# Gated DeltaNet stage of a two-layer trunk: silu through one Tanh, and inverse roots by Newton steps on GpSimd

## The reference, cut to what matters

```python
qkv = jax.nn.silu(causal_depthwise_conv(proj[..., :GDN_QKV_W], conv_w))
z = proj[..., GDN_QKV_W:GDN_QKV_W + GDN_VAL_W]
q = l2norm(q) * (GDN_DK ** -0.5)     # x * rsqrt(sum(x * x) + L2_EPS)
k = l2norm(k)
...
tmat = eye + a_low                   # beta * (k k^T) * decay below the diagonal
sol = triangular_solve(tmat, rhs)    # u, w
def step(s, inp):
    v_new = u_c - w_c @ s
    o_c = qd_c @ s + qk_c @ v_new
    s = s * dl_c + kd_c.T @ v_new
    return s, o_c
...
o = rmsnorm(o, o_norm) * jax.nn.silu(z)
```

## Time and profile before

| | us |
|---|---|
| median of 3 runs | 2728.78 (2727.26 to 2729.28) |
| profiled execution, its own time | 2729.88 |
| its span, first to last instruction | 2728.1 |
| mean granted clock of TensorE in it | 0.962 |
| PE busy | 2479.6 (91%) |
| DVE busy | 1671.6 (61%) |
| ACT busy | 1129.3 (41%) |
| POOL busy | 454.4 (17%) |
| the stage's later steps, each | 40.2 |
| its steps with a meta pass, each | 50.7 to 52.0 (steps 2 to 6) |

### The profile page before, as it was taken

How to read it: one execution, slowest core, us unless ns; L and a number is a source line. 1 busy time by engine, 2 the same in 40 slices (tenths; PEclk the granted TensorE clock), 3 DMA queues, 4 the chain that set the end, 5 groups by cost and what they waited for, 6 DMA issues and landing times. The chain is left out here.

```text
span 2728.1 us, 46465 instructions
## 1 busy us (share of the span) xinstructions
PE 2479.6 (91%) x17193; PEld 2186.3 (80%) x17193; DVE 1671.6 (61%) x3906; ACT 1129.3 (41%) x3326; POOL 454.4 (17%) x341
## 2 busy tenths in 40 slices
PE   5468888899999999999999689999998999999997
PEld 4467877789999999999999568878886777777775
DVE  4367777777777777777777333333333667666674
ACT  4244554544444444444444244423332333333332
POOL 0043343310000000000000012100000333323331
PEclk8689999999999999999999689999998999999998
DMA  6665454344544454444353067744456222222221
GB/s 188 199 211 171 157 189 154 118 144 156 180 141 133 157 172 158 133 155 141 125 175 100 20 216 254 249 161 143 172 201 235 105 71 87 88 71 78 70 71 49
DMA packets 274337, 395.36 MB, mean 145 GB/s; under 512 B 80066, under 2 KB 188178, under 8 KB 273714
## 3 DMA queue, kind: packets, MB, share of 16 engines
q1 hardware_dynamic: 241314, 371.25, 40.7%
q10 hardware_dynamic: 32800, 21.17, 2.6%
HBM read 268.95 MB, written 123.95 MB: 144 GB/s over the span
## 5 line engine op out<-in xcount | busy, mean ns | idle before, releaser
L1232 PE MATMUL p_psp<-xg,p_whi 128*128 128x264 f32 x4096 | 842.4, 295 | 24.4 <-POOL p_wlo L1181 17.2
L1232 PEld LDWEIGHTS p_psp<-xg,p_whi 128*128 128x128 f32 x4096 | 655.2, 191 | 28.6 <-issue 26.3
L1232 PE MATMUL p_psp<-xg,p_wlo 128*128 128x264 f32 x2048 | 606.8, 296 | 0.0
L1232 PEld LDWEIGHTS p_psp<-xg,p_wlo 128*128 128x128 f32 x2048 | 391.4, 191 | 0.0
L984 DVE SCALAR_TENSOR_TENSOR p_acc<-p_proj,p_taps,p_acc 128x528 f32<-128x528 f32 x288 | 244.7, 850 | 4.6
L1857 PE MATMUL first_q<-first_w,p_o 128*128 128x512 f32 (+1 forms) x864 | 206.1, 397 | 15.1 <-DVE first_w L1821 15.1
L2403 PE MATMUL first_q<-first_w,p_hT 128*128 128x512 f32 x720 | 194.3, 409 | 11.4 <-DMA p_hT<-hT_dram 11.4
L1857 PEld LDWEIGHTS first_q<-first_w,p_o 128*128 128x128 f32 (+1 forms) x864 | 156.6, 183 | 57.9 <-issue 13.6
L2403 PE MATMUL p_pso<-p_wo,p_oT 128*128 128x512 f32 x768 | 194.6, 404 | 7.9 <-DVE p_oT L2314 4.2
L865 ACT ACTIVATE p_sig<-p_sig 128x528 f32<-128x528 f32 x128 | 82.5, 645 | 282.0 <-DVE p_sig L986 282.0
L1857 PE MATMUL p_psz<-p_wk,p_o 128*128 128x512 f32 x768 | 181.3, 392 | 0.0
(11 more groups left out here) (264 smaller groups left out, 4637.2 us busy)
## 6 DMA issues: line engine op xcount, KB each, us to landing
p_whi<-w_dram SPq DMA_DIRECT2D x92, 512.0 KB, 4.0
p_wlo<-w_dram SPq DMA_DIRECT2D x92, 512.0 KB, 4.8
raw<-w_a_in SPq DMA_DIRECT2D x36, 512.0 KB, 6.6
w_dram<-p_whi SPq DMA_DIRECT2D x34, 512.0 KB, 3.9
w_dram<-p_wlo SPq DMA_DIRECT2D x34, 512.0 KB, 5.0
p_o<-hT_dram SPq DMA_DIRECT2D x34, 512.0 KB, 4.8
hT_dram<-p_hT SPq DMA_DIRECT2D x32, 512.0 KB, 3.4
p_hT<-hT_dram SPq DMA_DIRECT2D x30, 512.0 KB, 4.4
```

Of the source, the lines that this page charges most:

```text
L1232: ins = nc.tensor.matmul(ps_p[half_][:, 0:HALF], (w_hi, w_lo)[i][:, f, kc * P:(kc + 1) * P], xg[:, g % 2, j, kc, half_ * HALF:(half_ + 1) ...
```

## The change

Five things change, all within `gated_deltanet`.

- The sigmoid's three passes and the clamp are replaced by one pass of Tanh with scale 0.5 on ScalarE; the product becomes (tanh + 1) times x on VectorE, which is twice the silu. The factors of two are taken out later (0.25 with the squared norm of the keys, four times the epsilon, half the output gain). The products of f = 2 and f = 3 run on VectorE in every step, and the products' slots move: f = 0 from 11 to 10, f = 1 from 21 to 20, f = 2 from slot 0 of the next step to 23, f = 3 from 5 to 3.
- Inverse square roots are no longer Ln and Exp on ScalarE. VectorE writes a seed from the bits of the argument, and GpSimd does three Newton steps of four linked operations each (`inverse_root`): root_k for |k|, in slot 16 (18 in steps with a meta pass), with one more product; root_o for the outputs, in slot 12 (16). 1/|k|^2 becomes a reciprocal on VectorE.
- The scaling of the outputs becomes a stage of its own on ScalarE, slot 14 (18), and close and store move from 16 and 18 to 17 and 19 (20 and 22). The meta pass has root_o, scale, close and store in slots 1, 4, 6, 8, where norm, close and store stood in 0, 2 and 4.
- The roots lie in tiles of their own, one for each kind and pass (`root`, and `n2` for the squared norm).
- The meta pass's outputs lie in the PSUM bank `ps_t`, which also takes the transposes of the inverse, instead of `ps_o1`. PE's wait for the close of the meta pass moves from the second ks to the second left.

The diff, cut to its core:

```diff
-        TAPS = {7: (0, 0, (0, 1)), 8: (0, 0, (2, 3)), 9: (0, 0, (4,)), 13: (0, 1, (0,)), 14: (0, 1, (1,)),
-                16: (0, 1, (2,)), 18: (0, 1, (3,)), 19: (0, 1, (4,)), 20: (0, 2, (0, 1)), 21: (0, 2, (2, 3)), 22: (0, 2, (4,)),
-                1: (1, 3, (4,))}
-        SIGMOID = {9: (0, 0, (0,)), 10: (0, 0, (1, 2)), 19: (0, 1, (0,)), 20: (0, 1, (1, 2)), 22: (0, 2, (0,)),
-                   23: (0, 2, (1, 2)), 1: (1, 3, (0,)), 2: (1, 3, (1, 2))}
-        SILU = {11: (0, 0), 21: (0, 1), 0: (1, 2), 5: (1, 3)}
+        TAPS = {7: (0, 0, (0, 1)), 8: (0, 0, (2, 3)), 13: (0, 1, (0,)), 14: (0, 1, (1,)),
+                16: (0, 1, (2,)), 18: (0, 1, (3,)), 20: (0, 2, (0, 1)), 21: (0, 2, (2, 3))}
+        TANH = {9: (0, 0), 19: (0, 1), 22: (0, 2), 1: (1, 3)}
+        SILU = {10: (0, 0), 20: (0, 1), 23: (0, 2), 3: (1, 3)}
...
-                    put(2, "close", b[0], 0)
-                    put(4, "store", b[0], 0)
+                    put(1, "root_o", b[0], 0)
+                    put(4, "scale", b[0], 0)
+                    put(6, "close", b[0], 0)
+                    put(8, "store", b[0], 0)
...
-                put(16, "close", main, 0)
-                put(18, "store", main, 0)
+                put(20 if main.with_meta else 17, "close", main, 0)
+                put(22 if main.with_meta else 19, "store", main, 0)
...
                 for q in p:
+                    put(18 if q.with_meta else 16, "root_k", q, 0)
+                for q in p:
...
                 put(12, "norm", b[-1], 0)
+                put(16 if b[-1].with_meta else 12, "root_o", b[-1], 0)
+                put(18 if b[-1].with_meta else 14, "scale", b[-1], 0)
...
@@ -1062,14 +1047,19 @@
                                                               nD[par][:, p.which, c:c + 1], e_g[:, p.ix(c), :],
                                                               ALU.mult, ALU.mult)
                     last.then_inc(low_ready, 1)
+                    if not zero(p.first):
+                        dve.wait_ge(vs_ready, p.first)
+                    link(nc.vector.tensor_scalar(root[:, 0, p.which, 0, 0:n], squared, -0.5, None, ALU.mult))
+                    nc.vector.tensor_scalar(root[:, 0, p.which, 1, 0:n].bitcast(i32), squared.bitcast(i32), -0.5, float(ROOT_SEED),
+                                            ALU.mult, ALU.add).then_inc(norm_seeded, 1)
                 elif stage == "vs":
                     dve.wait_ge(v_ps, k + 1)
-                    dve.wait_ge(norm_ready, 2 * k + 2)
+                    dve.wait_ge(norm_ready, k + 1)
                     nc.vector.tensor_tensor(v_s[par][:, at, :], chunks(ps_t if p.meta else ps_k)[:, 0:n, :], bc(norm[:, p.which, 0:n], n),
                                             ALU.mult).then_inc(vs_ready, 1)
...
@@ -1116,8 +1106,11 @@
                 elif stage == "norm":
                     dve.wait_ge(state_ready, p.chunk + n)
                     dve.wait_ge(oss_ready, p.chunk + n)
-                    nc.vector.scalar_tensor_tensor(o_ms[:, 0:n], o_ss[:, 0:n], 1.0 / P, o_bias[par][:, p.which, 0:n],
-                                                   ALU.mult, ALU.add).then_inc(ms_ready, 1)
+                    link(nc.vector.scalar_tensor_tensor(o_ms[:, 0:n], o_ss[:, 0:n], 1.0 / P, o_bias[par][:, p.which, 0:n],
+                                                        ALU.mult, ALU.add))
+                    link(nc.vector.tensor_scalar(root[:, 1, p.which, 0, 0:n], o_ms[:, 0:n], -0.5, None, ALU.mult))
+                    nc.vector.tensor_scalar(root[:, 1, p.which, 1, 0:n].bitcast(i32), o_ms[:, 0:n].bitcast(i32), -0.5, float(ROOT_SEED),
+                                            ALU.mult, ALU.add).then_inc(ms_seeded, 1)
...
+            links = [0]
+
+            def link(ins):
+                links[0] += 1
+                ins.then_inc(pool_chain, 1)
+                pool.wait_ge(pool_chain, links[0])
+
+            def inverse_root(kind, p, last=None):
+
+                minus_half, y, t = (root[:, kind, p.which, x, 0:p.n] for x in range(3))
+                for turn in range(ROOT_STEPS):
+                    link(nc.gpsimd.tensor_tensor(t, y, y, ALU.mult))
+                    link(nc.gpsimd.tensor_tensor(t, t, minus_half, ALU.mult))
+                    link(nc.gpsimd.tensor_scalar(t, t, 1.5, None, ALU.add))
+                    step_done = nc.gpsimd.tensor_tensor(y, y, t, ALU.mult)
+                    if turn == ROOT_STEPS - 1 and last is not None:
+                        step_done.then_inc(last, 1)
+                    else:
+                        link(step_done)
+                return y
...
+                elif stage == "root_k":
+                    pool.wait_ge(norm_seeded, k + 1)
+                    y = inverse_root(0, p)
+                    nc.gpsimd.tensor_tensor(norm[:, p.which, 0:p.n], n2[:, p.which, 0:p.n], y, ALU.mult).then_inc(norm_ready, 1)
+                elif stage == "root_o":
+                    pool.wait_ge(ms_seeded, k + 1)
+                    inverse_root(1, p, last=ms_ready)
...
+                pool.sem_clear(pool_chain)
+                links[0] = 0
                 for slot in schedule(it, p, a, b, splitting):
                     for stage, q, index in slot.stages:
                         stage_of(stage, q, index, b)
-                    for q, item, f in slot.silu:
-                        if f >= 2 and splitting[1]:
-                            silu(q, item, f, b)
...
                     if index:
+                        if index == 1 and b and b[0].meta:
+                            pe.wait_ge(o_g_ready, b[0].number + 1)
...
-                        if index == 1 and p.with_meta:
-                            pe.wait_ge(o_g_ready, k)
```

More of the change, by code:

```diff
@@ L884, in stage_of @@
                     act.wait_ge(k_ps, k + 1)
+                    if not zero(k):
+                        act.wait_ge(scaled, k)
                     for c in range(n):
@@ L888, in stage_of @@
                     last.then_inc(k_squared, 1)
-                elif stage == "kk":
-                    l = lnk[:, p.which, 0:n]
-                    act.wait_ge(k_squared, k + 1)
-                    link(nc.scalar.activation(l, ssq[:, p.which, 0, 0:n], ACT.Ln, bias=cst[:]))
-                    if not zero(k):
-                        act.wait_ge(scaled, k)
-                    if not zero(p.first):
-                        act.wait_ge(vs_ready, p.first)
-                    nc.scalar.activation(rn2[:, p.which, 0:n], l, ACT.Exp, scale=-1.0).then_inc(norm_ready, 1)
-                    nc.scalar.activation(norm[:, p.which, 0:n], l, ACT.Exp, scale=0.5).then_inc(norm_ready, 1)
                 elif stage == "tokQ":
@@ L929, in stage_of @@
                         nc.scalar.activation(o_n[:, c, :], o_of(p, c), ACT.Copy,
-                                             scale=o_ms[:, c:c + 1]).then_inc(o_read, 1)
+                                             scale=root[:, 1, p.which, 1, c:c + 1]).then_inc(o_read, 1)
                 elif stage == "store":
@@ L1323, in stage_of @@
                         pe.wait_ge(qk_ready, k + 1)
+                        if p.meta and a and a[0].meta:
+                            pe.wait_ge(vs_ready, a[0].number + 1)
                         if p.leading:
```

126 lines of the change are left out of this document (49 added, 77 removed).

## The result

The changed kernel takes 2740.15 us (median of 5 runs, 2731.42 to 2745.34) against 2728.78 on the same chip: a ratio of 1.004, 95% interval 1.003 to 1.0051. The forecast of 2709.8 was wrong, on the wrong side of no change, and the measured time lies just past the end of its range (2740.0). The profiled execution of after is the lowest of its five runs (2731.42, span 2729.6), so the trace shows a loss of only 1.5 us in the span; what the other runs add is taken up with the first experiment.

What follows compares the result with a forecast made beforehand. PE's matmuls were taken to set the time, so only PE's waits could be won. Later steps -24, opening and steps 8, 9 -4, early +6, end +3 give -19; 2729.9 - 19 - 1.1 = 2709.8 us, range 2693 to 2740.

Steps and rivals of the forecast that it cites:

- three signs of being wrong: Links taking 0.4 us, the inverse's load waited for 22 times, or the early steps getting shorter.
- Later steps, -24: Steps 10 to 31: PE's waits for keys and state go, 1.1 us a step over 22 steps; bounds -11 to -31.
- the load of the inverse would not follow: Rival, chance 0.16: in later steps the inverse's DRAM load lands late, leaving some 0.3 us a step; 2727.
- The link, 0.28 us: One dependent small GpSimd operation of the inverse roots takes 0.28 us; bounds 0.18 and 0.51.
- The end, +3: Last step: 0.66 us from o_ms to first scaling becomes two seeds, 0.4 us, and 12 links, 3.4; bounds +2 and +5.
- Opening steps, -3: Steps 0 and 1: each saves two sigmoid passes and a clamp, partly taken back by VectorE's work; -1 to -6.
- Steps 8 and 9, -1: These two steps win half a microsecond each.
- Early steps, +6: Steps 2 to 7: per step -3.0 ScalarE, +2.3 VectorE, +1.7 GpSimd, so +1.0; bounds -11 to +33.
- ScalarE's relief: Early steps: waits for w and evacuations, and half of those for vT, go; -3.0 us a step.
- 310.6 + 38 s reaches 322.3 at s = 0.31, so 0.28 just fits: Early steps: 38 links of s us after a weight split ending at 310.6 must finish before the values' scaling at 322.3.
- 12 small operations: Early steps: VectorE's added squared norm, reciprocal and seed work, priced at 0.15 us each and a hand-off.
- The link is dear: Rival, chance 0.20: links cost more, nothing won at 0.43 us, 2746 at 0.47, about 2766 at 0.51.

Runs made afterwards that it cites:

- a0_again: The first experiment: the changed kernel run once more, nothing altered; 2740.48 us, ratio 1.0042.
- e1: The changed kernel with the outputs' root ahead of the keys' root in steps 8 and 9; 2732.23 us, ratio 1.0014.
- e6: The changed kernel with the main keys' seeds put behind the addition into p_X in early steps; 2734.36 us, ratio 1.0023.
- e9: The changed kernel with one Newton step instead of three and the main keys' seeds behind the addition into p_X; 2702.45 us, ratio 0.9908.
- e3: The changed kernel with root_o in slot 12 and the meta keys' root in 13, ahead of the weight splits; 2709.57 us, ratio 0.9933.
- e8: The kernel before the change with five idle linked VectorE operations ahead of the second addition into p_X in meta-pass steps; 2742.17 us, ratio 1.0056.
- e10: The changed kernel with e3's root order, plus qT product and solve rows 4, 5, 6 behind the first r in early steps; 2679.9 us, ratio 0.9824.
- e4: The changed kernel with one Newton step instead of three, so 14 links instead of 38; 2723.51 us, ratio 0.998.

## Why the prediction was wrong, point by point

The sum was to be -19 against the profiled execution; its span grew by 1.5, and the median lies 8.7 us above that execution. Two terms failed, the early steps by 13 us and steps 8 and 9 by 7; in a0_again, whose profile lies near its median, these stretches lost even 22.8 and 9.3. None of the three signs of being wrong that the prediction named came true: links of 0.4 us, an inverse waited for 22 times, shorter early steps.

- **Later steps, -24: right** (-25.2; 39.1 us each, as forecast). Keys and state left the waits of PE. That the load of the inverse would not follow, a rival, did not happen: after waits for it 3 times in 22 steps, 1.4 us in all.
- **The link, 0.28 us: right where nothing disturbs it** (12 links from 780.29 to 783.90 in step 13, 0.30 with one of them stretched by 0.25). The Trainium skill, "GPSIMD Engine Reference", section 4.1, led to an estimate of 0.38; the trace gives 0.28 alone, and 0.37 in the early step, where it is the waiting for VectorE and not the work that is longer (0.99 and 0.20 for the same operation).
- **The end, +3: right.** From `p_oms` to the first scaling 4.0 us (1555.35 to 1559.39) instead of 0.66, +3.4; 3.8 us had been forecast, and the rest of the span grew by 2.0.
- **Opening steps, -3, measured -1.1**: within the bounds given (-1 to -6).
- **Steps 8 and 9, -1: failed, +6.3.** I had looked at the root of the outputs in the later steps and in the early ones, and not in these two, where both roots stand in slot 16 and the keys' comes first (e1: -8 us in the median, and these steps back at 88.5).
- **Early steps, +6: this term failed; +19.4** (inside its own bounds, -11 to +33). The step that failed is the price of a wait. The term counts what PE waits for and takes its matmuls as fixed; TensorE's clock does not occur in it, though step 4 of before already ran at 0.97 and kept PE busy for 43.63 us instead of 42.56. PE's idle time did grow by 5.2 us, near the +6; the other 14.2 are busy time at the lower clock. That the idle time came out near is in part luck, since its parts did not. ScalarE's relief came as named and a little larger (20.3 us over w, the evacuations and vT; 18 had been forecast). The place was named too, "310.6 + 38 s reaches 322.3 at s = 0.31, so 0.28 just fits", and so was the contention; but 0.05 us a link for it was too little (0.09), the chain started 1.3 us later in the step, and I took what misses the values as the whole price. The seed, one of the "12 small operations" priced at 0.15 us, stands behind a whole weight split and holds `p_X` (e6 and e9). After the values there are still two qT products and a held product ahead of r, so r came 5.75 us later in the step, not the 1 us of my term: 58.61 (328.21 - 269.60) against 52.86 in the trace of before, of which 3.8 are the step's own growth.

With the order put right in two lines (e3) the six steps lose 4.0 us, the term of +6 nearly holds, and the median is 2709.57 where 2709.8 was forecast. There too it is luck in part: PE is busy for 6.9 us more than before the change and idle for 2.9 less. And it does not make the forecast right: the kernel as changed has the order that it has, and the order was there to be read. Of the rivals none was this one. "The link is dear" ended on the right side for half a reason: beside VectorE a link took 0.37, for which its own sum gives 38 x 0.06 - 0.7 = 1.6 us a step, half of the loss; at the end of the stage, where the links are alone, they cost what I had taken.

The held seed is the rule that the prediction cited from the Trainium skill ("SBUF — State Buffer", section "Who interferes with whom"): the engine that comes second is blocked for the whole of the other's instruction. The trace agrees, 1.16 us against 0.16 and the ends 0.03 us apart; I had applied it to GpSimd's links only, as a small addition to each, and not to the one small VectorE operation that PE waits behind.

Left open: the wider spread of the changed kernel's runs (2731 to 2745, before 2725 to 2730 beside them). Two profiles place the difference in steps 2, 3, 8 and 9, where the order was tight; what starts it was not found. Open too is what it takes for a wait to lower the clock: both waits do so in step 3 of after, but in e8 the longer wait for `p_X` does not in every step.

## What to carry to other kernels

Before a chain of linked small operations goes to a slow in-order engine, write down what stands ahead of it and behind it in that engine's queue, slot by slot, and at each change of phase: two lines of order were worth 31 us here, more than the 25 that the change won in the later steps. Price a small operation at the longest instruction that can hold it, not at its own length, and look at what is queued behind it. Look at PE's busy time too, and not only at its waits: most of the early steps' loss lay there. And a relief on one engine counts only once the next queue in line is opened too: moving three rows of VectorE won 25 us in the reordered kernel with the Tanh and nothing in the kernel before.

## What the runs showed of the hardware

A wait of PE costs more than its length where the granted clock falls behind it: in step 3 of after, to 0.50 in the 3 us in which its wait of 3.76 us for r ended, and to 0.62 in the 3 us behind a wait of 0.99 us for `p_X` (1.00 again from 278.6 and from 317.6 us). In steps 2 to 7 PE's busy time grew by 14.2 us with it, its idle time by 5.2. But the length of the wait alone does not decide it: e10 waits 1.3 us for the values in each step, and its step 3 stays at 1.00. And two causes that end in the same step do not add up: removing either (e4, e6) changed nothing, removing both won 20.5 us in six steps.
